# Attention layer of a decoder trunk: score products and search a unit sooner, score adds three places later, probability transposes seven places behind their logits, two probability buffers

## The reference

```python
def dsa_attention(q, k, v, q_idx, k_idx, w_idx, top_k):      # per block of 128 queries
    score = relu(einsum('bthd,bsd->bths', qib, k_idx))       # 8 index heads of 64
    score = einsum('bths,bth->bts', score, wb)
    score = where(admissible, score, -inf)
    _, sel = top_k(score, top_k)                             # 128 of up to 512 keys
    logits = einsum('bthd,btkhd->bthk', qb, k_sel) * scale   # 8 heads of 64
    probs = softmax(where(valid, logits, -inf))
    return einsum('bthk,btkhd->bthd', probs, v_sel)

def conv_sparse_attn_mixer(h, cos, sin, w_in, conv_w, w_out, top_k):
    sc_b, sc_c, sc_x, q, k, v, q_idx, k_idx, w_idx = split(h @ w_in)
    y_conv = sc_b * causal_depthwise_conv(sc_c * sc_x, conv_w)
    q, k, q_idx, k_idx = rope of each on its first 16 of 64 dims
    return concat([y_conv, dsa_attention(...)]) @ w_out
```

## Time and profile before

| | us |
|---|---|
| three runs | 2189.42, 2183.52, 2184.07; median 2184.07 |
| profiled execution, its own time | 2185.86 |
| span of the profile | 2184.1 |
| mean granted TensorE clock | 0.989 |
| busy in the span: PE, DVE, ACT, POOL | 2099.6, 1043.7, 776.2, 311.8 |
| HBM traffic | 87 GB/s over the span |

### The profile page before, as it was taken

One profiled execution on the slowest core, in us unless ns is written; L12 is line 12 of the kernel. 1 busy time (PEld: TensorE's weight loads), 2 busy tenths in 40 slices (PEclk: granted clock), 3 DMA queues, 4 the chain that ended last, 5 costly groups with the idle time before them and its releaser, 6 DMA issues.

```text
span 2184.1 us, 25568 instructions
## 1 busy us (share of the span) xinstructions
PE 2099.6 (96%) x9528; PEld 1714.6 (79%) x9528; DVE 1043.7 (48%) x1534; ACT 776.2 (36%) x1083; POOL 311.8 (14%) x390
## 2 busy tenths in 40 slices
PE   7999999988889999999999999998999999999997
PEld 6888888766677888888788888877788887888886
DVE  4444444468844444432344443255666554444422
ACT  4333322322563333322333332244645543333221
POOL 1000000433121000000000000026656310000001
PEclk9999999999999999999999999999999999999999
DMA  4333322453112333332233332222221223333321
GB/s 170 98 97 97 112 93 65 126 134 87 49 49 87 96 96 96 103 106 89 78 96 96 96 114 93 83 71 77 78 79 56 77 88 91 98 98 97 108 94 50
DMA packets 60875, 200.38 MB, mean 92 GB/s; under 512 B 12640, under 2 KB 12672, under 8 KB 60800
## 3 DMA queue, kind: packets, MB, share of 16 engines
q1 hardware_dynamic: 58592, 199.24, 29.5%
q10 hardware_dynamic: 2208, 0.13, 0.1%
HBM read 188.58 MB, written 2.38 MB: 87 GB/s over the span
## 4 chain that ended last, share of the span: by engine, by line
PE 80%; DVE 6%; POOL 4%; ACT 3%; DMA 3%; issue 2%; SPq 1%; DVEq 0%; POOLq 0%; ACTq 0%
PE prod L482 25%; PE prod L483 25%; PE prod L484 25%; DMA blk<-blocks 2%; POOL rows_tmp L1593 2%; POOL rows L1596 2%; PE misc L696 1%; ACT w_hi L839 1%; PE misc L599 1%; DVE w_lo L1117 1%; DVE top L1237 1%; ACT silu_g L946 0%; DVE raw L1230 0%; PE misc L575 0%; SPq L450 0%
## 5 line engine op out<-in xcount | busy, mean ns | idle before, releaser
L1117 DVE TENSOR_TENSOR w_lo<-raw,w_hi 128x1024 fp32r<-128x1024 f32 (+1 forms) x290 | 382.2, 1318 | 790.3 <-ACT w_hi L839 789.7
L482 PE MATMUL prod<-h_hi,w_hi 128*128 128x512 f32 x1856 | 746.3, 402 | 1.2 <-DVE w_lo L1117 0.9
L484 PE MATMUL prod<-h_hi,w_lo 128*128 128x512 f32 x1856 | 727.0, 392 | 0.0
L483 PE MATMUL prod<-h_lo,w_hi 128*128 128x512 f32 x1856 | 727.0, 392 | 0.0
L839 ACT ACTIVATE w_hi<-raw 128x1024 fp32r<-128x1024 f32 (+1 forms) x317 | 356.1, 1123 | 595.2 <-PE prod L484 583.7
L482 PEld LDWEIGHTS prod<-h_hi,w_hi 128*128 128x128 f32 x1856 | 351.6, 189 | 75.4 <-issue 4.4
L484 PEld LDWEIGHTS prod<-h_hi,w_lo 128*128 128x128 f32 x1856 | 350.9, 189 | 75.4
L483 PEld LDWEIGHTS prod<-h_lo,w_hi 128*128 128x128 f32 x1856 | 351.6, 189 | 71.4 <-issue 3.2
L482 PE MATMUL prod<-a_hi,w_hi 128*128 128x512 f32 x704 | 278.1, 395 | 0.0
L484 PE MATMUL prod<-a_hi,w_lo 128*128 128x512 f32 x704 | 278.1, 395 | 0.0
L483 PE MATMUL prod<-a_lo,w_hi 128*128 128x512 f32 x704 | 278.1, 395 | 0.0
(11 more groups left out here) (255 smaller groups left out, 1823.5 us busy)
## 6 DMA issues: line engine op xcount, KB each, us to landing
raw<-in_w SPq DMA_DIRECT2D x253, 512.0 KB, 3.6
raw<-in_wd SPq DMA_DIRECT2D x64, 704.0 KB, 4.1
blk<-blocks SPq DMA_DIRECT2D x8, 512.0 KB
x<-in_x SPq DMA_DIRECT2D x8, 256.0 KB, 5.8
k_dup<-act_f SPq DMA_DIRECT2D x8, 256.0 KB, 4.2
k_dup<-silu_g SPq DMA_DIRECT2D x8, 256.0 KB, 4.4
out<-y_out SPq DMA_DIRECT2D x8, 256.0 KB, 2.3
silu_g<-g_rows SPq DMA_DIRECT2D x7, 256.0 KB, 4.8
```

What stands on the lines that cost most here:

```text
L482: pe.matmul(bank, wh, hi, start=first and k == 0, stop=False)
L483: pe.matmul(bank, wh, lo, start=False, stop=False)
L484: ins = pe.matmul(bank, wl, hi, start=False, stop=last and k == tiles_n - 1)
L1117: dve.tensor_tensor(w_lo[:, n % 2, 0:w], raw[:, n % 4, 0:w], w_hi[:, n % 2, 0:w].bitcast(F32), ALU.subtract).then_inc(lo_ready, 1)
```

## The change

Five things are edited. The score products start in unit 7 instead of 8 and the search rounds in unit 9 instead of 10, at the same places. VectorE adds a score product three slots after the slot of its product instead of one. The attention pairs start one slot later (17*8 + 7), with the transposes 7 places behind the logits instead of 5, values 10 instead of 8 and mix 12 instead of 10; so pairs start on average 77/16 slots apart instead of 80/16. Probabilities go to two buffers in turn, `silu_g` and `hf`, and an exponential waits for the transposes of two pairs before. The side product of unit 1 is issued at place 7 of unit 2 instead of place 3, and VectorE takes it in at place 7 instead of 5.

```diff
         for k in (3, 6):
-            if u >= 8 and idx:
+            if u >= 7 and idx:
                 out[u * KT + k] = [idx.pop(0)]
         for k in (2, 4, 5, 7) if 14 <= u < 18 else (2, 5, 7):
-            if u >= 10 and top:
+            if u >= 9 and top:
                 out[u * KT + k] = [top.pop(0)]
...
-ATT_SLOT = 17 * KT + 6
-ATT_STEPS = {"logits": 0, "scale": 3, "turn": 5, "values": 8, "mix": 10}
+ATT_SLOT = 17 * KT + 7
+ATT_STEPS = {"logits": 0, "scale": 3, "turn": 7, "values": 10, "mix": 12}
...
+SCORE_LAG = 3
...
-        probs = silu_g
+        probs = (silu_g, hf)
...
-                        ins = pe.transpose(misc[:, 1 + e, c * P:(c + 1) * P], probs[:, e, c * P:(c + 1) * P],
+                        ins = pe.transpose(misc[:, 1 + e, c * P:(c + 1) * P], probs[p % 2][:, e, c * P:(c + 1) * P],
...
-                    if k == (7 if u == 1 else 3):
+                    if k == (7 if u <= 2 else 3):
                         ev_side_pe(u - 1)
...
-                    if p >= 1:
-                        act.wait_ge(turned, p)
+                    if p >= 2:
+                        act.wait_ge(turned, p - 1)
                     for e in range(2):
-                        ins = act.activation(probs[:, e, 0:w], relu_s[:, e, 0:w], ACT.Exp, bias=amax_n[:, e:e + 1],
+                        ins = act.activation(probs[p % 2][:, e, 0:w], relu_s[:, e, 0:w], ACT.Exp, bias=amax_n[:, e:e + 1],
                                              accum_out=asum[:, e:e + 1])
...
-                        ins = act.activation(probs[:, e, 0:w], probs[:, e, 0:w], ACT.Copy, scale=arcp[:, e:e + 1])
+                        probs_e = probs[p % 2][:, e, 0:w]
+                        ins = act.activation(probs_e, probs_e, ACT.Copy, scale=arcp[:, e:e + 1])
...
-                elif k == (7 if u == 0 else 5):
+                elif k == (7 if u <= 1 else 5):
                     ev_side_dve(u)
...
-                    ev_extra_dve([e for e in extras.get(u * KT + k - 1, []) if e[0] == "idx"])
+                    ev_extra_dve([e for e in extras.get(u * KT + k - SCORE_LAG, []) if e[0] == "idx"])
```

## The result

The changed kernel takes 2150.28 us (median of 4 runs, 2149.76 to 2151.78) against 2184.2 for the kernel before on the same chip (4 runs, 2183.52 to 2189.42): ratio 0.9841, 95% interval 0.9824 to 0.9858, 33.9 us less. The forecast was 2149, range 2138 to 2165. The profiled execution took 2149.76 us with a span of 2148.0, at a mean granted clock of 0.994 where it was 0.989.

The account below looks back on a forecast made before the run. PE was taken as the bound, busy 96% of the span, with time lost only where it waits in the attention layer's projection units. 3.8 + 25 + 17 - 8 - 3 = 35 us off the median 2184.1 gave 2149, range 2138 to 2165.

Parts of the forecast that it names:

- Part A: Moving unit 1's side product to place 7 of unit 2 saves 3.8 us: idle 2.0 plus slow matmuls 1.7.
- Part B: Score products and search a unit sooner, adds three places later: 25.0 us lost today, 8 us of it remaining.
- the 8 us left: Loss remaining after sooner search and later adds, from adds meeting POOL's `w_lo`: about 6 us idle, 8 us lost.
- the ratio of 1.3 from idle to lost: Today's lost time over PE's idle time, (3.8 + 25 + 17) / (2 + 17.4 + 15.8), applied to 6 us idle.
- The `k_dup` DMAs: Stacking DMAs awaited by the evacuation two units on: up to 0.6 us in three units, within the 8 us.
- Part C: Later transposes, values and mix with two probability buffers: 17 us lost today, 3 us of it remaining.
- some 8 us of PE work for a chain of 6.5: Attention, logits to transposes: PE has some 8 us of work during a 6.5 us chain, removing waits of 602 to 646 us.
- the 3 us left over for the transposes: Waits remaining in the attention pairs at 545 to 602 us: 3 us, bounds 0 and 11.
- The first: Units 9 to 13: VectorE becomes the bound, adds waiting out both POOL instructions, 3.7 us each unit; 2162 us, chance 0.22.
- The second: Everything is absorbed by slack, leftover under 3 us; 2140 us, chance 0.13.
- the third: Attention chain is set by VectorE's queue, not its length; 545 to 602 us keeps its 11; 2162 us, chance 0.06.
- the fourth: Slower: on ScalarE an exponential waiting for VectorE's mask stands ahead of the next unit's weight split; 2204 us, chance 0.04.

Follow-up runs that it names:

- lag_one: Changed kernel with the adds one place behind their product again, score products and search still a unit sooner; 2170.78 us, ratio 0.9923 to the kernel before.
- turn_five: Changed kernel with the earlier attention slots and steps (transposes 5, values 8, mix 10), two probability buffers kept; 2166.2 us, ratio 0.9907 to the kernel before.
- pool_waits: Changed kernel with POOL, in units 8 to 13, starting `w_lo` only after the previous unit's place-6 adds; 2144.24 us, ratio 0.981 to the kernel before.
- scores_alone: Kernel before with only score products and search a unit sooner and the adds three places later; 2163.84 us, ratio 0.99.
- units_late: Changed kernel with score products from unit 8 and search from unit 10 again, adds still lagged; 2149.08 us, ratio 0.9827 to the kernel before.
- values_twelve: Changed kernel with values 12 and mix 14 places behind the logits instead of 10 and 12; 2144.09 us, ratio 0.9807 to the kernel before.
- attention_alone: Kernel before with only the later attention slots and steps and two probability buffers; 2171.11 us, ratio 0.9933.
- one_buffer: Changed kernel with one probability buffer, exponentials waiting for the previous pair's transposes, slots unchanged; 2154.35 us, ratio 0.9857 to the kernel before.

## Why the prediction was right, point by point

**What bounds the kernel, and the price of today's waits.** 3.8 + 25 + 17 = 45.8 us were said to be lost in the three places. lag_one and turn_five give B and C back whole, so these were the right causes. The 25 us were well priced: pool_waits, with 0.2 us of waits left in the second stretch, is 24.1 us shorter there than the kernel before.

**Part A, 3.8 us.** Measured 3.9, in the changed kernel and alone. No price behind it appeared. But only the 2.0 us of idle time are sure: the 1.7 for slow matmuls are not lost in scores_alone, which waits just as long there at a granted clock of 1.00.

**Part B, 25 - 8 = 17 us.** Measured 18.4. The mechanism was the forecast's: the evacuation slips because the place-6 adds meet POOL's `w_lo`. pool_waits shows it. Of the 8 us left, the idle part was well sized (6 forecast, 5.4 measured), the ratio of 1.3 from idle to lost was not: taking 5.2 of the 5.4 away brought 5.7 us. That ratio came from a kernel whose stretches with waits show 0.88 to 0.94 granted. The changed kernel's longest wait here is 2.1 us, and all its stretches show 1.00. The forecast didn't split B between the sooner start and the lag; by units_late the sooner start has no part in it. The trace shows a side effect that the forecast had wrong: L1235 was to stay near 2.3 us, but the mask now comes after adds that have waited for POOL themselves, and averages 0.29. The adds were to take longer where they read the place-6 tile: their mean goes from 1.21 to 1.57 us at 512 columns and from 1.05 to 1.22 at 256, but not at 384 (1.08 and 1.06). The mask:

```profile
L1237 DVE TENSOR_TENSOR raw<-raw,consts 128x128 f32<-128x128 f32 x2 | 0.6, 293 | 0.1
```

**The `k_dup` DMAs,** priced at up to 0.6 us in three units, made one wait: VectorE waited 3.1 us for the landing ahead of unit 8's evacuation, and 0.75 us of it reached PE.

```profile
443.87 0.69 DVE L1307 TENSOR_TENSOR silu_g<-prod,cosT 128x512 f32<-128x512 f32 x1 [3.14 <-DMA k_dup<-silu_g]
...
445.21 1.13 PE L600 MATMUL misc<-hf,consts 128*128 128x512 f32 x2 [0.75 <-DVE hf L1308]
```

**Part C, 17 - 3 = 14 us.** Measured 13.3 in the whole and 14.8 alone; the 1.5 us between them are the cost of the sooner search, which the forecast didn't have. The two places removed the waits at the transposes, to 0.4 us, more than said. The step that failed is "some 8 us of PE work for a chain of 6.5", which stopped at the transposes: the copy behind them has three places to the values product, and nothing was said of it. 5.5 us are waited there, and the sum was close by luck: the 3 us left over for the transposes stood in its place, and the places freed more than was said. The second buffer had no price of its own in the sum; it is worth 5.6 us.

**The rivals.** The first (VectorE as the bound, 2162) had the mechanism but not the size; in the changed kernel the place-6 adds of units 9 to 13 lose 0 to 2.3 us a unit (1.63, 3.03, 1.26, 3.77 and 2.57 us for two that take about 1.0, 1.3, 1.3, 1.5 and 1.5 alone), not for 3.7 in each. By the Trainium skill, page SBUF — State Buffer, section on the two separate sides, a VectorE instruction with two SBUF inputs and a GpSimd (POOL) instruction that reads SBUF exclude each other for a whole instruction. The trace agrees: 3.77 us for two adds of 0.75, 1.57 us on average against 0.88 when `w_lo` stays away. The second (2140) needed what pool_waits adds. The third is excluded by the third stretch, the fourth showed only as 0.4 us in values_twelve.

**The sum.** 35 us forecast for the layer; 35.6 from the first side product to the layer's end, 36.1 in the span, 33.9 by the medians.

## What to carry to other kernels

For each product that PE waits for, write down what stands ahead of its producer on that engine's queue, and move what nobody waits for behind it: that alone was worth 18 us here with not one instruction less. When a wait is taken out of a chain, follow the chain to its next step as well, since the two places given to the transposes uncovered a wait three places on. Where VectorE and POOL meet in the SBUF, let the one that has slack wait for the other on a semaphore: PE never waited for POOL's `w_lo` in pool_waits, and the wait on it was worth 5 to 6 us.

## What the runs showed of the hardware that was not expected

A wait of PE of the same length can cost clock or not. The same wait at the same place, 1.97 us in the kernel before, 1.98 in attention_alone and 1.99 in scores_alone, was followed by a granted clock of 0.79, 0.79 and 1.00 over the next 7 to 8 us, and the time from there to the next rotation was 8.05, 8.06 and 6.43 us. Waits of up to 2.2 us left it at 1.00 in every stretch of the layer in the changed kernel, while the stretches of the earlier trace rows with waits of up to 3.1, 4.6 and 3.0 us showed 0.93, 0.88 and 0.94; scores_alone waited up to 3.5 us in its third stretch at 1.00. What decides isn't told apart by these runs.

One stretch with the same code in it took 97.0 us in the changed kernel and 95.9 in three others (one_buffer, turn_five, values_twelve: unit 3 to unit 16), with waits of 5.4 and 3.9 to 4.0 us in sum. The first of them is for the `k_dup` landing, 0.75 against 0.34 to 0.42 us, and the later ones are spread otherwise: 2.1, 1.2, 0.5 and 0.9 us, where the others have six of at most 1.0. scores_alone has the pattern of the changed kernel (0.6, 2.1, 1.2, 0.5 and 0.9); whether the landing sets off the rest was not tried.
